# Sums and spreads of the head norms: four heads at a time on quarters of the TensorE array

## The reference

```python
ret = head_group_norm(retention(...), ret_norm_g)          # 4 heads, after retention
gla_o = rms_norm(gla(...), gla_norm_g)                     # 4 heads, after gated linear attention
fox_o = forgetting_attention(rms_norm(q, q_norm_g),        # 4 heads of q and 4 of k, before attention
                             rms_norm(k, k_norm_g), v, f)
```

## Time and profile before

| what | value |
|---|---|
| time, median of 3 runs | 3088.19 us (3084.37 to 3089.88) |
| the profiled execution's own time | 3088.36 us |
| its span | 3086.6 us |
| PE busy | 97% of the span |
| DVE, ACT, POOL busy | 34%, 35%, 38% |
| DMA | 102 GB/s on average |
| TensorE clock, mean | 0.985 of full |
| start to start at full clock, split weights, 128x512 | 0.23 us |
| the same, 128x256 | 0.12 us |
| start to start of two scalings on DVE (line 2019) | 0.66 us |

### The profile page before, as it was taken

How to read it: one execution, slowest core, us unless ns; L and a number is a source line. 1 busy time by engine, 2 the same in 40 slices (tenths; PEclk the granted TensorE clock), 3 DMA queues, 4 the chain that set the end, 5 groups by cost and what they waited for, 6 DMA issues and landing times.

```text
span 3086.6 us, 36366 instructions
## 1 busy us (share of the span) xinstructions
PE 2998.0 (97%) x15435; PEld 2510.3 (81%) x15435; DVE 1057.1 (34%) x1828; ACT 1082.9 (35%) x1651; POOL 1176.3 (38%) x502
## 2 busy tenths in 40 slices
PE   7999999999999999999999999989999999999999
PEld 4888788898888888778888888978888876788887
DVE  2533462255554532232143220452110255531102
ACT  3424333243332433432234332333222265432221
POOL 1422144434445432224435444334444332344442
PEclk9999899999999999999999999999999999999999
DMA  6332253335555422223323333323333222233332
GB/s 210 103 89 62 83 177 96 89 116 179 189 188 174 110 69 62 55 64 100 96 82 104 100 93 94 96 71 98 97 100 94 86 75 62 62 96 96 96 94 77
DMA packets 523798, 315.30 MB, mean 102 GB/s; under 512 B 15954, under 2 KB 496884, under 8 KB 523380
## 3 DMA queue, kind: packets, MB, share of 16 engines
q1 hardware_dynamic: 523636, 312.98, 34.2%
HBM read 310.84 MB, written 2.10 MB: 101 GB/s over the span
## 4 chain that ended last, share of the span: by engine, by line
PE 92%; DVE 4%; ACT 2%; DMA 1%; issue 0%; SPq 0%; ACTq 0%; DVEq 0%
PE b L413 21%; PE b L415 20%; PE b L414 20%; PE o L413 5%; PE o L415 5%; PE o L414 5%; DMA raw<-in_w_in_dram 1%; PE b L454 1%; PE b L455 1%; PE b L456 1%; PE b L558 1%; PE o L730 1%; DVE SA L2097 1%; ACT aT L1290 1%; PE t L498 1%; PE s L624 1%
## 5 line engine op out<-in xcount | busy, mean ns | idle before, releaser
L2478 POOL TENSOR_TENSOR lo<-raw,hi 128x1024 fp32r<-128x1024 f32 (+1 forms) x492 | 1174.1, 2394 | 1872.1 <-ACT hi L1159 1871.7
L413 PE MATMUL b<-HH,hi 128*128 128x512 f32 x1776 | 707.8, 399 | 15.1 <-ACT aT L1290 10.5
L415 PE MATMUL b<-HH,lo 128*128 128x512 f32 x1776 | 695.1, 391 | 0.0
L414 PE MATMUL b<-HL,hi 128*128 128x512 f32 x1776 | 695.1, 391 | 0.0
L1159 ACT ACTIVATE hi<-raw 128x1024 fp32r<-128x1024 f32 (+1 forms) x492 | 508.6, 1039 | 443.9 <-DMA raw<-in_w_down_dram 106.0
L413 PEld LDWEIGHTS b<-HH,hi 128*128 128x128 f32 x1776 | 335.7, 189 | 92.4 <-issue 19.6
L415 PEld LDWEIGHTS b<-HH,lo 128*128 128x128 f32 x1776 | 335.5, 189 | 71.6
L414 PEld LDWEIGHTS b<-HL,hi 128*128 128x128 f32 x1776 | 335.7, 189 | 69.5 <-issue 1.0
L2205 DVE TENSOR_TENSOR CB<-CB,b 128x512 f32<-128x512 f32 x82 | 56.4, 687 | 453.2 <-PE b L415 439.9
L413 PE MATMUL b<-FH,hi 128*128 128x512 f32 (+1 forms) x572 | 209.3, 366 | 0.0
L415 PE MATMUL b<-FH,lo 128*128 128x512 f32 (+1 forms) x572 | 208.6, 365 | 0.0
(11 more groups left out here) (420 smaller groups left out, 4616.2 us busy)
## 6 DMA issues: line engine op xcount, KB each, us to landing
raw<-in_w_ada_dram SPq DMA_DIRECT2D x96, 512.0 KB, 4.9
raw<-in_w_up_dram SPq DMA_DIRECT2D x88, 512.0 KB, 3.9
raw<-in_w_in_dram SPq DMA_DIRECT2D x80, 512.0 KB, 4.2
raw<-in_w_mg_dram SPq DMA_DIRECT2D x48, 512.0 KB, 3.7
raw<-in_ffn_w_gate_dram SPq DMA_DIRECT2D x44, 512.0 KB, 3.8
raw<-in_ffn_w_up_dram SPq DMA_DIRECT2D x44, 512.0 KB, 3.8
raw<-in_w_down_dram SPq DMA_DIRECT2D x32, 512.0 KB, 3.9
raw<-in_ffn_w_down_dram SPq DMA_DIRECT2D x32, 512.0 KB, 3.9
```

Source lines behind the costliest of these rows:

```text
L413: e.matmul(out, wh, xh, start=start and k == 0, stop=False)
L414: e.matmul(out, wh, xl, start=False, stop=False)
L415: mm = e.matmul(out, wl, xh, start=False, stop=stop and k == last)
L2478: e.tensor_tensor(t["lo"][:, s, 0:w], K.raw[:, s, 0:w], t["hi"][:, s, 0:w].bitcast(F32), ALU.subtract).then_inc(*m.lo.up(n))
```

## The change

**Sums.** `colsq` goes, and `head_sums` comes. The roles are swapped: the squares are moved through the array, 128 positions at a time, and the weights are 32 columns of a constant (`pick`) in which column j is one and the others zero. The four heads of a group go to the four column quarters of the array (output partitions 32i to 32i+31). Four passes j = 0 to 3 add up in PSUM, so that row 32i+j holds the sums of positions 128j to 128j+127 of head i. One call has 16 matmuls with 128x32 weights and 128 moved columns. The result is 128x128, of which 16 rows are of use, four in each quarter.

**Spreads.** `head_rows` takes the place of `spread` for these norms. The weights are column 32i+j of the identity, on 32 partitions, read 128 times; row quarter i of the array gets the 32 rows of head i as moved data. One call has 16 matmuls of 32 rows by 128 columns of weights and 128 moved columns, four banks in turn. They are plain matmuls, not transposes.

**Groups.** Per layer there are four calls of `head_sums` (retention, fox q, fox k, gla) in place of 16 of `colsq`, and four of `head_rows` (retention, fox heads 0 and 1, fox heads 2 and 3, gla) in place of 16 of `spread`. The fox root is split into one for q and one for k. Roots and reciprocals work on 128x128. The squares of all four heads are kept, so ACT no longer waits for PE to free a buffer. `fqS` lies on the place of `fk`, `fkS` on that of `fv`, and two waits guard this.

The diff, cut:

```diff
+    out["pick"] = np.broadcast_to(np.arange(36) == 3, (128, 36)) * 1.0
...
+HEAD_BANKS = ("t0", "t1", "s0", "s1")
...
-    def colsq(self, sq, st, col, ready, key):
-        e, q = self.e, self.q
-        q.wait_ge(*ready)
-        for r in range(4):
-            mm = e.matmul(st[:, col + r:col + r + 1], sq[:, r * 128:r * 128 + 128], self.t["ones"][:, 0:1], start=True,
-                          stop=True)
-        mm.then_inc(*self.m.stat.up(key))
+    def head_sums(self, squares, b, ready, key):
+        e, q, t = self.e, self.q, self.t
+        q.wait_ge(*ready, self.free[b])
+        for j in range(4):
+            for i, sq in enumerate(squares):
+                mm = e.matmul(self.bank[b][32 * i:32 * i + 32, 0:128], t["pick"][:, 3 - j:35 - j],
+                              sq[:, j * 128:j * 128 + 128], start=(j == 0), stop=(j == 3))
+        mm.then_inc(*self.m.stat.up(key))
+
+    def head_rows(self, parts, ready, keys):
+        e, q, ident = self.e, self.q, self.t["ident"]
+        q.wait_ge(*ready, *[self.free[b] for b, _, _ in parts])
+        for j in range(4):
+            for b, r, row in parts:
+                c = 32 * r + j
+                r = slice(32 * r, 32 * r + 32)
+                mm = e.matmul(self.bank[b][:, j * 128:j * 128 + 128], bc(ident[r, c:c + 1], 128), row[r, :], start=True,
+                              stop=True)
+        mm.then_inc(*self.m.stat.up(*keys))
...
@@ PE, ret_attention
-            if n >= 6 and (n - 6) % 4 == 0:
-                h = (n - 6) // 4
-                self.colsq(t["retS"][:, h % 2, :], bank["t1"], 4 * h, (m.aattn.at("rsq", l, h), free["t1"]),
-                           ("rsum", l, h))
+            if n == len(steps) + 2:
+                self.head_sums([t["retS"][:, h, :] for h in range(4)], "t1", [m.aattn.at("rsq", l, h) for h in range(4)],
+                               ("rsum", l))
...
+        self.head_rows([(HEAD_BANKS[h], h, t["retR"]) for h in range(4)], [m.vattn.at("rr", l)],
+                       [("rspread", l, h) for h in range(4)])
...
@@ PE, fox_inputs
-            yield from self.project(w, 3600 + 128 * i, key, lambda key=key: m.vtake.at(*key))
-            if i >= 1:
-                self.fox_sum(l, i - 1, st)
+            tile = self.project(w, 3600 + 128 * i, key, lambda key=key: m.vtake.at(*key))
+            for j, _ in enumerate(tile):
+                if (i, j) == (4, 0):
+                    self.fox_sums(l, 0)
+                yield None
...
+            for j, _ in enumerate(rows):
+                if (c, j) == (0, 1):
+                    self.fox_sums(l, 1)
+                yield None
...
@@ PE, fox_norm
-            for i in (h, 4 + h):
-                b = ("t0", "t1", "s0", "s1")[2 * h % 4 + i // 4]
-                self.spread(t["RS2"][:, 4 * i:4 * i + 4], b, m.vattn.at("fr", l), ("fspread", l, i))
-                self.free[b] = m.vattn.at("fn", l, i)
+            if h % 2 == 0:
...
+                self.head_rows(parts, [m.vattn.at("fr", l, 0), m.vattn.at("fr", l, 1)],
+                               [("fspread", l, i) for i in (h, 4 + h, 1 + h, 5 + h)])
...
@@ PE, gla_attention
-        self.gla_sum(l, 0)
-        self.gla_sum(l, 1)
-        yield None
-        self.gla_sum(l, 2)
-        yield None
-        self.gla_sum(l, 3)
+        yield None
+        yield None
+        self.head_sums([t["glaS"][:, h, :] for h in range(4)], "t1", [m.aattn.at("gsq", l, h) for h in range(4)],
+                       ("gsum", l))
...
@@ ACT
-        self.rstd(bank["t1"], 16, 128, m.stat.at("rsum", l, 3), t["RS"][:, 0:16], m.aattn.up(("rsd", l)))
+        self.rstd(bank["t1"], 128, 128, m.stat.at("rsum", l), t["retR"][:, :], m.aattn.up(("rsd", l)))
...
+            if i == 4:
+                self.rstd(self.bank["b2"], 128, 128, m.stat.at("fsum", l, 0), t["foxR"][:, 0, :], m.aattn.up(("fsd", l, 0)))
...
-                self.rstd(self.bank["b2"], 32, 128, m.stat.at("fsum", l, 7), t["RS2"][:, 0:32], m.aattn.up(("fsd", l)))
+                self.rstd(self.bank["b2"], 128, 128, m.stat.at("fsum", l, 1), t["foxR"][:, 1, :], m.aattn.up(("fsd", l, 1)))
...
@@ DVE, fox_inputs
+            if i == 4:
+                self.fox_roots(l, 0)
+            q.wait_ge(m.atake.at("fsq", l, i), m.stat.at("fsum", l, 0) if i >= 4 else None)
...
+    def fox_roots(self, l, k):
+        R = self.t["foxR"][:, k, :]
+        self.q.wait_ge(self.m.aattn.at("fsd", l, k))
+        self.e.reciprocal(R, R).then_inc(*self.m.vattn.up(("fr", l, k)))
```

More of the change, by code:

```diff
@@ L660, in fox_inputs @@
         m, t, bank = self.m, self.t, self.bank
-        w, st = self.w, bank["b2"]
+        w = self.w
         parts = []
@@ L669, in fox_inputs, with fox_sums @@
             key = ("fq", l, i) if i < 4 else ("fk", l, i - 4)
-            yield from self.project(w, 3600 + 128 * i, key, lambda key=key: m.vtake.at(*key))
-            if i >= 1:
-                self.fox_sum(l, i - 1, st)
-        for c in range(2):
[L674 to L678, removed]
-        yield None
-    def fox_sum(self, l, j, st):
-        m = self.m
-        self.colsq(self.t["foxS"][:, j % 2, :], st, 4 * j, (m.atake.at("fsq", l, j), self.free["b2"]), ("fsum", l, j))
+            tile = self.project(w, 3600 + 128 * i, key, lambda key=key: m.vtake.at(*key))
[3 more added lines that the diff above has]
+                yield None
+        for c in range(2):
+            rows = self.project_rows(w, 4624 + 256 * c, [("fv", l, c, u) for u in range(2)],
+                                     lambda u, c=c: m.atake.at("fv", l, c, u))
+            for j, _ in enumerate(rows):
+                if (c, j) == (0, 1):
+                    self.fox_sums(l, 1)
+                yield None
+        yield None
+    def fox_sums(self, l, k):
+        m, t = self.m, self.t
+        heads = [(h + 2 * k) % 4 for h in range(4)]
+        self.head_sums([t[("fqS", "fkS")[k]][:, h, :] for h in heads], "b2",
+                       [m.atake.at("fsq", l, 4 * k + h) for h in heads], ("fsum", l, k))
+        self.free["b2"] = m.aattn.at("fsd", l, k)
     def fox_norm(self, l):
@@ L687, in fox_norm @@
         for h in range(4):
-            for i in (h, 4 + h):
-                b = ("t0", "t1", "s0", "s1")[2 * h % 4 + i // 4]
-                self.spread(t["RS2"][:, 4 * i:4 * i + 4], b, m.vattn.at("fr", l), ("fspread", l, i))
-                self.free[b] = m.vattn.at("fn", l, i)
+            if h % 2 == 0:
+                parts = []
+                for i in (h, 4 + h, 1 + h, 5 + h):
+                    b = HEAD_BANKS[2 * (i % 2) + i // 4]
+                    parts.append((b, (i % 4 + i // 4 * 2) % 4, t["foxR"][:, i // 4, :]))
+                self.head_rows(parts, [m.vattn.at("fr", l, 0), m.vattn.at("fr", l, 1)],
+                               [("fspread", l, i) for i in (h, 4 + h, 1 + h, 5 + h)])
+                for i in (h, 4 + h, 1 + h, 5 + h):
+                    self.free[HEAD_BANKS[2 * (i % 2) + i // 4]] = m.vattn.at("fn", l, i)
             yield None
@@ L820, in gla_attention @@
             yield None
-        self.gla_sum(l, 0)
-        self.gla_sum(l, 1)
         yield None
-        self.gla_sum(l, 2)
         yield None
-        self.gla_sum(l, 3)
+        self.head_sums([t["glaS"][:, h, :] for h in range(4)], "t1", [m.aattn.at("gsq", l, h) for h in range(4)],
+                       ("gsum", l))
         free["t1"] = m.aattn.at("gsd", l)
         yield None
+        self.head_rows([(HEAD_BANKS[h], h, t["glaR"]) for h in range(4)], [m.vattn.at("gr", l)],
+                       [("gspread", l, h) for h in range(4)])
         for h in range(4):
-            b = f"t{h % 2}"
-            self.spread(t["RS"][:, 4 * h:4 * h + 4], b, m.vattn.at("gr", l), ("gspread", l, h))
-            free[b] = m.vattn.at("GO", l, h)
+            free[HEAD_BANKS[h]] = m.vattn.at("GO", l, h)
             yield None
[L835 to L838, removed]
     def gated(self, l, which):
@@ L1343, in fox_inputs @@
             yield from self.tile()
-            q.wait_ge(m.dense.at(*key), m.stat.at("fsum", l, i - 2) if i >= 2 else None)
-            e.activation(t["foxS"][:, i % 2, :], self.bank[self.K.where.get(key, "b0")][:, :],
+            if i == 4:
+                self.rstd(self.bank["b2"], 128, 128, m.stat.at("fsum", l, 0), t["foxR"][:, 0, :], m.aattn.up(("fsd", l, 0)))
+            q.wait_ge(m.dense.at(*key))
+            e.activation(t[("fqS", "fkS")[i // 4]][:, i % 4, :], self.bank[self.K.where.get(key, "b0")][:, :],
                          ACT.Square).then_inc(*m.atake.up(("fsq", l, i)))
@@ L1457, in gla_attention @@
         for h in range(4):
-            q.wait_ge(m.attn.at("go", l, h), m.stat.at("gsum", l, h - 2) if h >= 2 else None)
-            e.activation(SQ[:, h % 2, :], bank[GLA_BANKS[h]][:, :], ACT.Square).then_inc(*m.aattn.up(("gsq", l, h)))
+            q.wait_ge(m.attn.at("go", l, h))
+            e.activation(SQ[:, h, :], bank[GLA_BANKS[h]][:, :], ACT.Square).then_inc(*m.aattn.up(("gsq", l, h)))
             yield None
```

(2 more changed lines are left out.)

47 lines of the change are left out of this document (22 added, 25 removed).

## The result

| kernel | median (lowest to highest), us | ratio to before (95%) |
|---|---|---|
| before, measured beside it | 3089.03 (3084.37 to 3091.15), 4 runs | |
| changed | 3063.94 (3061.66 to 3066.36), 4 runs | 0.9919 (0.9906 to 0.9932) |

What follows compares the result with a forecast made beforehand. PE was taken as the bound (busy 97% of the span, 92% of the wait chain). Gains of twice (6.3 + 0.5) + 3.4 + 2.9 + 3.0 + 1.8 = 24.7 us gave 3063.5 us, range 3056 to 3080.

Steps and rivals of the forecast that it cites:

- The overlap of the quarters: In the new sums and spreads, four array quarters work side by side, 8 records each; forecast case's chance 0.64.
- S: Time on PE of one new group of 16 sums, forecast at 1.2 us, or 2.0 at gla's low clock.
- R: Time on PE of one new group of 16 spreads, forecast at 1.3 us, or 2.0 at gla's low clock.
- The 0.86 us of work: Within a group, each quarter's 8 records at 0.107 us, all four quarters side by side.
- the allowance for the changes of form: Idle time for changing array tiling around a group: 0.17 us ahead of the first load and as much behind the last.
- The rival of two quarters at once: In the new groups only two quarters overlap, S and R 2.0 us, total 3077 us; chance 0.19.
- Part 3: Each layer up to the last k tile: nine column sums (7.5 us) go, one S comes; gain 6.3 us.
- Part 4: From there to retention's spreads: table load leaves the chain, 7.1 us becomes 6.6, PE idles 1.3; gain 0.5 us per layer.
- Part 5: Retention's spreads through fox's: three R (3.9 us) replace 7.3 and 6.8, clock staying at 2.4 GHz; gain 3.4 and 2.9 us.
- The second fox group: Fox's second group of spreads needs banks back from DVE: 2.7 us of scalings fit PE's 2.9; wait costed at 0.1, left out.
- Part 6: gla's norm: chain shortened by four buffers and the new groups at low clock; gain 3.0 us in layer 0, 1.8 in layer 1.

Runs made afterwards that it cites:

- experiment 3: Changed kernel with only the spreads reordered, head as the outer loop so each row quarter serves four matmuls running: 3082.2 us, 0.9985 to the kernel before.
- experiment 4: Changed kernel with the sums in two pairs of quarters, heads 0 and 1 in turn, then 2 and 3: 3059.24 us, single execution; a group took 1.48 us.

## Why the prediction came out

**The overlap of the quarters** was the step on which all hung, and it was right: four at once, S = 1.01 for 1.2 and R = 1.10 for 1.3, and 2.0 each at half clock, as forecast. The 0.86 us of work was exact; the allowance for the changes of form was too large. Records show 0.09 us extra ahead of a group of sums and 0.09 behind, where I had taken 0.17 twice, from a row with only 2 moved columns behind each of its 32 loads. The rival of two quarters at once, with a chance of 0.19, described the other order of the loops: with the head outside, two work at once, and with the spreads alone in that order the whole gain shrinks to 0.15% (experiment 3). The Trainium skill (TensorE: Matmul & The Clock Gate, Part 3: Packing small matmuls) lets a weight load overlap running matmuls only when its row group differs; here column quarters, which share all rows, overlap fourfold, and in both orders that were tried for both, column quarters cost less than row quarters.

**Part 3** (6.3 us in each layer, 6.8 up to the first row of v): 6.5 and 7.3. No idle time appeared ahead of the new sums of q, of retention and of k. S smaller by 0.2 gives 7.2, which is layer 1; what layer 0 lacks was not traced.

**Part 4** had a right mechanism and one term that failed in layer 0. The idle time was forecast at 1.3 us: 1.16 and 1.25 in layer 1, but 2.26 and 2.72 in layer 0, because the weight DMA took 4.94 and 5.40 us there, for the 4.10 I had carried over from one execution. The second trace of the kernel before has 4.50 at this place, the other kernels that have the change 3.92 to 5.45, and in layer 1 both traces of both kernels have 3.7 to 3.9. So a part of the difference is there between executions of one program; what lengthened the rest was not tried.

**Part 5** took it that the clock stays up behind retention's spreads. It did in three of the four places of the two traces, and fell in layer 0 of the first, where 1.4 us are missing (1.7 gained in that stretch, for 3.2 in the other trace). The second fox group did not wait: DVE's fourth scaling started at 240.21 and the group at 241.15, with no idle time.

**Part 6**: last square to gate tile, forecast 5.5 us behind the square's end, measured 371.00 - 365.44 = 5.56. The gain up to that tile was 1.9 and 3.1 us in layer 0 (forecast 3.0), 2.3 and 3.4 in layer 1 (1.8). The chain itself, from the square of bank t to the tile, came out as forecast: 6.64 us in all four places of the two traces, for 9.67 and 9.66 in layer 0 and 8.39 and 9.57 in layer 1 before (there ACT waited 0.66 us for a buffer in the first trace and 1.47 in the second), so 3.0, 3.0, 1.8 and 2.9. What the gains differ by lies ahead of the chain. The 1.9, for one: PE's common rows came 7.3 us earlier than before, but the square only 6.2 (364.36 for 370.58); ACT had waited 3.58 us for DVE in the gate step, for 3.01 before, which is about half of it. The step that failed stands behind it: I ended the sum at the gate tile, and the tile itself runs longer at half clock when the norm ahead of it is shorter. That took 0.3 to 1.8 us of each place back.

**The total** (3063.5 for 3063.94) is closer than its parts deserve, which is luck. S and R were 0.2 too dear (some 2 us over the groups at full clock), which made up for gla and for the clock in layer 0, and 4 us in the last attention, outside every term, stand against 0.6 to 3.7 lost between 1213 and 1324.

## What to carry to other kernels

Small fp32 matmuls that use a quarter of the array's rows or columns run four at a time if the four quarters are taken in turn (that neighbours differ is not enough, experiment 4); put the loop over quarters innermost, or a group takes about two and a half times as long. Then look at what the shorter group leaves behind: a chain of square, sum, root, reciprocal and spread is a hole of some us on TensorE, and later matmuls that need nothing from it belong in it, both for their own time and because the clock then stays up. If one engine in a chain interleaves it with other work, move all of the chain ahead of that work, not its first step alone.

## What was not expected

- **How far TensorE runs ahead.** With four matmuls in a row for each quarter, a new quarter starts directly behind the fifth of the eight records of the one before, 0.467 us (sums) and 0.555 us (spreads) behind its first. This rests on three orders of the sums and two of the spreads.
- **A change of form costs 0.2 us for a group**, as start-to-start time ahead and behind together.
- **The clock is not a function of the idle time ahead.** 2.26 us of idle were followed by half clock, 2.72 by full clock, in two executions of one program. Such stretches gave up to 3 us of difference between the two pairs of traces (1213 to 1324) and largely cancelled over the span, so an effect under some 3 us is read from common rows in the trace, not from the total.
